# Ten of twelve column groups of the mixer's first product computed in channels, with standing weights

## The reference

```python
z = h @ w_in                                   # 256 x 2048 times 2048 x 6144
hy = dwconv3(z[..., :3072], hy_short_w, hy_short_b)
x0, x1, v = jnp.split(hy, 3, axis=-1)
y_a = x0 * two_sided_fftconv(v * x1, h_fwd, h_bwd, hy_bias)
gb, gc, xv = jnp.split(z[..., 3072:], 3, axis=-1)
y_b = gb * dwconv3(gc * xv, sc_conv_w)
return jnp.concatenate([y_a, y_b], axis=-1) @ w_out
```

## Time and profile before

| | us |
|---|---|
| median of 3 runs | 2268.76 (2268.59 to 2268.84) |
| span of the profiled execution | 2266.9 |
| TensorE busy | 2255.3 (99%) |
| VectorE busy | 1675.5 (74%) |
| ScalarE busy | 1332.9 (59%) |
| DMA read | 534.6 MB, 239 GB/s |

### The profile page before, as it was taken

One profiled execution on the slowest core, in us unless ns is written; L12 is line 12 of the kernel. 1 busy time (PEld: TensorE's weight loads), 2 busy tenths in 40 slices (PEclk: granted clock), 3 DMA queues, 4 the chain that ended last, 5 costly groups with the idle time before them and its releaser, 6 DMA issues.

```text
span 2266.9 us, 26633 instructions
## 1 busy us (share of the span) xinstructions
PE 2255.3 (99%) x10625; PEld 1873.7 (83%) x10625; DVE 1675.5 (74%) x2025; ACT 1332.9 (59%) x1775; POOL 104.5 (5%) x138
## 2 busy tenths in 40 slices
PE   9999999999999999999999999999999999999998
PEld 7778888888888888888888888888888888888887
DVE  6676864887788788787878788778788685456664
ACT  6455444766666666666666666666666564444443
POOL 0000000000000000000000000000000010000000
PEclk9999999999999999999999999999999999999999
DMA  9454455899998999886578999989888645643343
GB/s 358 167 174 162 164 186 186 289 291 272 287 303 265 277 292 267 283 282 236 219 281 240 287 289 261 285 281 277 270 281 258 240 152 223 244 172 149 148 163 116
DMA packets 77132, 542.63 MB, mean 239 GB/s; under 512 B 8682, under 2 KB 9013, under 8 KB 13968
## 3 DMA queue, kind: packets, MB, share of 16 engines
q1 hardware_dynamic: 61568, 429.58, 50.2%
q0 software_dynamic: 15296, 111.23, 22.7%
q10 hardware_dynamic: 144, 0.12, 0.0%
HBM read 534.60 MB, written 6.29 MB: 239 GB/s over the span
## 4 chain that ended last, share of the span: by engine, by line
PE 98%; DVE 2%; issue 0%; ACT 0%; ACTq 0%; POOLq 0%; POOL 0%
PE P L359 95%; PE P L362 3%; DVE low L626 0%; DVE R_h L614 0%; DVE R_f L611 0%; DVE R_f_r L611 0%; DVE R_g L614 0%; DVE X L614 0%; ACT R_h L502 0%; ACT EV L533 0%; DVE st L614 0%; DVE R_f L708 0%; ACT X L502 0%; DVE X L611 0%; ACTq L2710 0%
## 5 line engine op out<-in xcount | busy, mean ns | idle before, releaser
L626 DVE TENSOR_TENSOR low<-raw,hi 128x1024 fp32r<-128x1024 f32 (+3 forms) x694 | 813.4, 1200 | 290.7 <-ACT hi L507 286.4
L507 ACT ACTIVATE hi<-raw 128x1024 fp32r<-128x1024 f32 (+3 forms) x694 | 704.5, 1040 | 463.5 <-PE P L359 309.5
L359 PE MATMUL P<-hi,R_h 128*128 128x512 f32 (+2 forms) x2944 | 944.2, 392 | 0.6 <-DVE R_h L614 0.6
L359 PE MATMUL P<-hi,R_f_r 128*128 128x512 f32 x2480 | 791.4, 391 | 0.1
L359 PEld LDWEIGHTS P<-hi,R_h 128*128 128x128 f32 x2944 | 552.3, 188 | 116.4 <-issue 5.8
L359 PE MATMUL P<-low,R_h 128*128 128x512 f32 (+2 forms) x1472 | 570.2, 387 | 0.0
L359 PEld LDWEIGHTS P<-hi,R_f_r 128*128 128x128 f32 x2480 | 465.6, 188 | 96.3 <-DVE R_f_r L611 0.3
L359 PE MATMUL P<-low,R_f_r 128*128 128x512 f32 x1240 | 482.5, 389 | 0.0
L626 DVE TENSOR_TENSOR low<-R_f,hi 128x1024 fp32r<-128x1024 f32 x226 | 267.7, 1221 | 82.9 <-ACT hi L507 82.2
L359 PEld LDWEIGHTS P<-low,R_h 128*128 128x128 f32 x1472 | 276.7, 188 | 54.7 <-issue 2.6
L359 PEld LDWEIGHTS P<-low,R_f_r 128*128 128x128 f32 x1240 | 233.0, 188 | 47.1
(11 more groups left out here) (229 smaller groups left out, 1406.2 us busy)
## 6 DMA issues: line engine op xcount, KB each, us to landing
raw<-in_w_d SPq DMA_DIRECT2D x128, 1024.0 KB, 7.2
R_f<-in_w_u POOLq DMA_DIRECT2D x84, 1024.0 KB, 10.5
raw<-in_w_u SPq DMA_DIRECT2D x72, 1024.0 KB, 5.6
raw<-in_w_z SPq DMA_DIRECT2D x45, 1024.0 KB, 4.9
raw<-in_w_i SPq DMA_DIRECT2D x36, 1024.0 KB, 4.9
R_f<-in_w_u SPq DMA_DIRECT2D x28, 1024.0 KB, 6.9
X<-in_w_u SPq DMA_DIRECT2D x28, 1024.0 KB, 8.7
raw<-in_w_mo SPq DMA_DIRECT2D x16, 1024.0 KB, 4.9
```

Of the source, the lines that this page charges most:

```text
L359: return self.e.matmul(o, l, r, start=start, stop=stop, skip_group_check=True)
L507: self.e.activation(hi, raw, ACT.Copy).then_inc(*self.inc("high_made", ("high", k, d)))
L626: self.e.tensor_tensor(low, raw, hi.bitcast(f32), ALU.subtract).then_inc(*self.inc("low_made", *lows))
```

## The change

Groups 0 and 1 (gc) stay as they were, but `evac` multiplies with the square of the norm's factor, since xv then comes without one. For the other ten groups a weight tile holds one block of 128 columns over all 16 k (`laid_out`). `column_product` lets 128 x 128 pieces of the weights stand: for each k the high weights meet both parts of all tokens in one instruction of 512 columns (`H_both`: 256 of `HH`, 256 of `HL`), and the low weights meet the high part in one of 256. A tile fills one bank with channels on the partitions; its two halves have to be added. `column_pair` does two tiles. `gathered` copies the right halves to SBUF on ScalarE, adds the left ones on VectorE, and multiplies with `r_row`, the norm's factors along a row (not for xv). `r_row` is made once by `norm_diagonal` and `norm_spread` (two small products). No transposes of EV follow. `conv(..., apart=True)` issues the centre taps at once and the side taps one step later. A pair has four steps, two of which its own work takes.

```diff
+Z_ROWS = 2
+PAUSES = 1,
+    def column_product(self, b, wh, wl, j, ks, x_ready, free, *done):
+        m = self.m
+        o = m.P[b]
+        for k in ks:
+            self.wait_ge(x_ready)
+            self.wait_ge(("low", j, k // 4))
+            both, high = m.H_both[:, :, 256 * k:256 * k + 256], m.HH[:, k, :]
+            if k == 0:
+                self.wait_ge(free)
+            if k < 15:
+                self.mm(o[:, :], wh[:, k, :], both, k == 0, False)
+                last = self.mm(o[:, 0:256], wl[:, k, :], high, False, False)
+            else:
+                self.mm(o[:, 0:256], wl[:, k, :], high, False, False)
+                last = self.mm(o[:, :], wh[:, k, :], both, False, True)
...
+    def norm_spread(self, b, k, ready, free, done):
...
+        for t in range(2):
+            last = self.mm(m.P[b][:, 128 * t:128 * t + 128], m.EV[k][:, 256:384], m.EV[k][:, 128 * t:128 * t + 128], True, True)
...
 class Act(Engine):
+    def gathered(self, k, banks, row, ready, row_ready, free, done):
+        self.wait_ge(free)
+        for d, b in enumerate(banks):
+            self.wait_ge(ready[d])
+            self.copy(self.m.EV[k][:, 256 * d:256 * d + 256], self.m.P[b][:, 256:512], (done, "copied", d))
...
 class Dve(Engine):
+    def gathered(self, k, banks, row, ready, row_ready, free, done):
+        m = self.m
+        o = m.EV[k]
+        for d, b in enumerate(banks):
+            part = o[:, 256 * d:256 * d + 256]
+            self.wait_ge((done, "copied", d))
+            self.tt(part, m.P[b][:, 0:256], part, ALU.add, (done, "half", d))
+        if row is not None:
+            self.wait_ge(row_ready)
+            self.wait_ge((done, "half", 1))
+            z = v3(o[:, :], 2)
+            self.tt(z, z, row.unsqueeze(1).to_broadcast([128, 2, 256]), ALU.mult, done)
...
+    def column_pair(kind, c):
+        banks, products = pair(), []
+        for d in range(2):
+            j, wh, wl = take("w_z")
+            wh, wl = v3(wh, 16), v3(wl, 16)
+            done = ("product", j, 1)
+            for part, ks in enumerate((range(0, 4), range(4, 8), range(8, 12), range(12, 16))):
+                whose = {1: [("used", j, 0)], 3: [done, ("used", j, 1)]}.get(part, [])
+                E.column_product(banks[d], wh, wl, j, ks, list(h_m), bank_free[banks[d]], *whose)
+                if part in PAUSES:
+                    step()
+            products.append(done)
+            release(j, done)
+            step()
+        rest = []
+        later.extend([lambda: rest.append(mixer_columns(kind, c, banks, products)), lambda: rest[0]()])
...
     for n, kind in enumerate(kinds):
-        banks, done = gemm("w_z", HH, HL, h_m, 16, 512, steps=2)
-        flush()
+        if n < Z_ROWS:
+            banks, done = gemm("w_z", HH, HL, h_m, 16, 512, steps=2)
+            flush()
...
+            continue
+        for c in (0, 2):
+            column_pair(kind, c + 4 * (n % 2))
         if n == 7:
             flush_all()
-        ks, ms = evac(banks, done, scale_m=list(r1_m))
-        later += [nop] * {0: 4, 1: 1, 8: 1, 9: 1, 10: 1}.get(n, 0)
-        for c in (0, 2):
-            later.append(lambda kind=kind, c=c + 4 * (n % 2), ks=ks, ms=ms: mixer_turn(kind, c, ks, ms))
```

More of the change, by code:

```diff
@@ L746, in gate, with norm_diagonal @@
         self.tt(o, z, g, ALU.mult, done)
+    def gathered(self, k, banks, row, ready, row_ready, free, done):
+        m = self.m
+        o = m.EV[k]
[8 more added lines that the diff above has]
+            self.tt(z, z, row.unsqueeze(1).to_broadcast([128, 2, 256]), ALU.mult, done)
+    def norm_diagonal(self, k, ready, free, done):
+        m = self.m
+        self.wait_ge(free)
+        self.e.memset(m.EV[k][:, 256:384], 1.0).then_inc(*self.inc("dve_done"))
+        self.wait_ge(ready)
+        self.tt(m.r_square, m.R1, m.R1, ALU.mult, (done, "square"))
+        for t in range(2):
+            self.ts(m.EV[k][:, 128 * t:128 * t + 128], m.ident[:, :], m.R1[:, t:t + 1], None, ALU.mult, done)
     def v_times_k(self, fc, g, ks, ready, free, before, done):
@@ L1686, in conduct, with conv @@
     g0_m, g1_m = [None] * 8, [None] * 8
-    def conv(zs, dsts, ws, biases, ready, frees):
+    def conv(zs, dsts, ws, biases, ready, frees, apart=False):
         done = mark("conv")
         E.centre(zs, dsts, ws, biases, ready, frees, done)
+        ends = [(done, d) for d in range(len(zs))]
+        if apart:
+            return ends, lambda: E.side_taps(zs, dsts, ws, done)
         E.side_taps(zs, dsts, ws, done)
-        return [(done, d) for d in range(len(zs))]
+        return ends
     def gate(o, z, g, ready, free=None):
@@ L1697, in gate, with row_columns, norm_diagonal, norm_spread @@
         return done
-    def mixer_columns(kind, c, b, turned):
-        z = v3(P[b][:, :], 2)
+    def row_columns(c, b, turned):
+        done = mark("gc")
+        E.copy_out(G0[:, c:c + 2, :], v3(P[b][:, :], 2), turned, list(h_m), done)
+        g0_m[c] = g0_m[c + 1] = done
+        bank_free[b] = [done]
+    norm_m = {}
+    def norm_diagonal():
+        norm_m["k"] = k = ev(hold=True)
+        norm_m["diagonal"] = done = mark("diagonal")
+        norm_m["square"] = (done, "square")
+        E.norm_diagonal(k, [list(r1_m), id_m[1]], ev_free[k], done)
+    def norm_spread():
+        b, k, done = bank(), norm_m["k"], mark("spread")
+        norm_m["row"] = mark("row")
+        E.norm_spread(b, k, norm_m["diagonal"], bank_free[b], done)
+        let_go(k, done)
+        E.copy_out(m.r_row, P[b][:, 0:256], done, None, norm_m["row"])
+        bank_free[b] = [norm_m["row"]]
+    def mixer_columns(kind, c, banks, products):
+        k, done = ev(hold=True), mark("gathered")
+        by_row = kind != "xv"
+        E.gathered(k, banks, m.r_row if by_row else None, products, norm_m["row"], ev_free[k], done)
+        for d in range(2):
+            bank_free[banks[d]] = [(done, "half", d)]
+        whole = done if by_row else (done, "half", 1)
+        z = v3(EV[k][:, :], 2)
+        zs = [z[:, d, :] for d in range(2)]
         if kind in ("x1", "v", "x0"):
             base = {"x0": 0, "x1": 8, "v": 16}[kind]
-            zs = [z[:, d, :] for d in range(2)]
             ws = [[m.SW[n](base + c + d) for n in range(3)] for d in range(2)]
```

72 lines of the change are left out of this document (43 added, 29 removed).

## The result

| | before | after |
|---|---|---|
| median of the runs | 2268.77 us (2268.59 to 2268.84) | 2294.11 us (2292.99 to 2295.28) |
| span of the profiled execution | 2266.9 us | 2292.9 us |
| mean granted clock of TensorE | 0.999 | 0.994 |

The ratio is 1.0112 with a 95% interval of 1.0099 to 1.0125: 25.3 us slower. The forecast was 15.5 us slower, with a range up to 2291. The sign was right, the size was not, and the time lies outside the range. The four runs lie within 2.3 us; those of the kernel before lie within 0.25 us here, and within 0.5 to 1.7 us in the larger sets that stand beside the experiments, so that differences of 1 to 2 us between single runs say little.

The account below looks back on a forecast made before the run. TensorE's queue was taken as the bound, as long as VectorE and ScalarE deliver. On the 2266.9 us span, -4.6 + 14.7 + 5.4 = +15.5 gave 2282.4, plus 1.9 for the median: 2284 us, range 2271 to 2291.

Parts of the forecast that it names:

- TensorE's own work, -4.6: TensorE's queue in the mixer: 8.8 us of transposes less, 4.2 and 0.3 us added, a 0.3 us wait gone.
- The turns: Two turns of four transposes removed in each of ten groups, 20 x 0.44 us: 8.8 us saved on TensorE.
- the extra starts: 32 more product starts in each of ten groups, at 0.347 us a pair: +4.2 us in all.
- the operand in two runs: 512-column product reading two runs of 256: taken at the plain 0.227 us, at worst +8.4 us in all.
- (d): Rival: weight loads lie bare on TensorE's path, 60 us more, 2325 to 2345 us; chance 0.02.
- `norm_spread`, +0.3: Two added 128-column products on TensorE for the norm's row, 0.3 us with their start.
- The burst, +14.7: All four kernel transforms between tiles 31 and 32: TensorE waits for VectorE's kernel parts and banks, 14.7 us.
- The walk of the queues: VectorE's and TensorE's work timed item by item from tile 26, with idle VectorE pieces; gave the 14.7 us stall.
- `y_back`, +5.4: First `y_back` waits 4.9 us for the last spectrum product, and a bank ahead of it 0.4 us: 5.4 us.
- (a): Rival: VectorE and ScalarE keep up everywhere, only TensorE's own sum stays, 2264.2 us; chance 0.09.
- (b): Rival: the kernel transforms' burst costs 5.2 to 8.7 us and `y_back` nothing, 2269.4 to 2272.9 us; chance 0.14.
- (c): Rival: split tiles late in groups 6 to 11, or double-run product costs 8.4 us: 2291 to 2300 us; chance 0.07.

Follow-up runs that it names:

- e8: The kernel before the change, with each of the mixer's 24 turns of four transposes made twice into the same bank: 2279.13 us.
- e11: Changed kernel with `norm_spread`, first `y_back` and centre taps later, kernel transforms spaced out, and the last product of spectra one step later: 2266.94 us.
- e7: Changed kernel with the 512-column product reading one run (high parts of two k) in place of two runs of 256: 2292.42 us.
- e1: Changed kernel with `norm_spread` moved from the middle of tile 5 to the middle of tile 7, nothing else: 2289.42 us.
- e6: Changed kernel with ScalarE's centre taps issued together with the side taps, behind the next weight split in place of ahead of it: 2284.99 us.
- e5: Changed kernel with 34 idle TensorE products ahead of the second kernel transform and 29 ahead of the third: 2295.85 us.
- e3: Changed kernel with the first `y_back` moved back by two steps of the inserted work: 2293.61 us.
- e4: Changed kernel with `norm_spread` two tiles later, an added step per pair to bring kernel transforms one by one, and first `y_back` two steps later: 2278.80 us.

## Why the prediction was right or wrong

**What bounds the kernel, and the direction.** Right: TensorE's queue sets the time, and VectorE had no room where the change leans on it.

**TensorE's own work, -4.6.** Mis-sized: it is -2.7. The turns were priced right (8.8 forecast, 8.7 by e8). The pair of products was not: taken as 0.347 us, it is 0.352 or 0.353 in most tiles (5.65 us a tile in place of 5.55), so that the extra starts cost about 6 us (8.8 - 2.7) and not 4.2. The two products of `norm_spread` are in that figure: they are four records, and in e11 put the products behind them off by 0.45 us in place of the 0.3 forecast. I had named the operand in two runs as the unknown; e7 clears it. In the kernel before three products also come each 0.69 us in some stretches in place of the 0.68 of the earlier trace rows, so one pair of rows was too narrow a base. What makes them 1 to 2% slower is not settled; by e7 it is not the operand, and how busy the other engines are does not explain it.

The rival with bare weight loads (d) fell. The changed kernel's 640 loads for the 256-column products show 189 ns each in the page's groups, and a pair of products with its two loads comes each 0.352 us, less than its two loads laid end to end (0.378). The rule of the Trainium skill that the prediction quotes ("TensorE: Matmul & The Clock Gate"; it stands in the section "The mechanism") would have them bare; this trace disagrees. The same section also lets TensorE pull a load ahead when it goes to the background weight buffer, which the prediction left out.

**`norm_spread`, +0.3.** The failed step, worth 4.6 us. I priced its two products and did not ask when their operand is ready. With this step put right alone (e1, 2289.42 us) the time lies inside the forecast's range. In the kernel before TensorE needs nothing of the norm until the first turn at 43.41 us; `norm_spread` stands some 5 us ahead of that, and the diagonal is made at 40.3 us, because the tokens' transfer, their squares, GpSimd's and VectorE's small steps and two low parts come first. VectorE's rows:

```profile
36.22 0.16 DVE L687 TENSOR_REDUCE st<-st 128x2 f32<-128x8 f32 x1 [4.22 <-ACT EV L565]
...
37.90 2.35 DVE L664 TENSOR_TENSOR low<-raw,hi 128x1024 fp32r<-128x1024 f32 x2
...
40.33 0.47 DVE L657 TENSOR_SCALAR EV<-ident,st 128x128 f32<-128x128 f32 x2
```

**The burst, +14.7.** The walk of the queues was right to 0.2 us. Counted from the start of transform 1 (27.75 in the walk, 201.58 in the trace), transform 2 was due after 9.25 us and came after 9.33; transform 3 was due after 17.45 and came after 17.60; the pieces of 2 us were there, and e6 shows their cause. Then transforms 3 and 4 took 5.3 us and not the 2.7 of full speed, and tile 32 began slow: 17.5 in place of 14.7. e5 shows that this piece is the clock's. The forecast had no term for it anywhere.

**`y_back`, +5.4.** Close, by luck, since two errors stood against each other: VectorE was ready 81.8 us after the end of tile 32 (forecast 81.9), but TensorE came 0.9 us later than forecast, since its tiles are slower, so the wait was 3.9 and not 4.9; no bank was waited for ahead of it; and the slow clock added 2.4 us. What would cure it was not seen: a later `y_back` alone gains nothing (e3); the piece of VectorE's work has to move behind the adds (e11).

**The chances.** The case with everything hidden (a) and the one with half the burst (b) did not happen. (c) had the right time, 2291 to 2300, for a reason that did not occur: neither late low parts nor the operand, but the clock and `norm_spread`. Term by term, the mark is 9.8 us later than the sum had it (25.3 against 15.5): 4.6 at `norm_spread`, 2.8 in the burst, 0.9 at `y_back` and 1.9 in the products make 10.2. The last 0.4 us of difference are not accounted for. The two steps that failed are the readiness of `norm_spread`'s operand and a clock taken as full behind every wait; the latter alone is about 7 us of it (1.8, 2.8 and 2.4).

## What to carry to other kernels

A change that takes steps out of a loop also takes away the slots in which other work was placed: check where every inserted item now falls, for its operand (is it made yet?) and for its bank (who reads it, and behind what in that engine's queue?). If a wait appears, look at what stands in the queue of the engine waited for; moving the waiter alone may only hand the wait to the next one. And a wait of a few us on TensorE can cost more than its length: here 0.6 us of slow work came with each us waited at `y_back` and at `norm_spread`, and 0.3 in the burst, while waits of 2.24 us (e3), 2.51 us (e7) and 2.60 us (e4) cost their length alone.

## What the hardware showed that I had not expected

After TensorE had been idle from 203 us, its granted clock was 1.00 until 206 us, 0.92 in the next 2 us, and then 0.50. It rose behind transform 2, while TensorE waited again (0.87 and 0.98), fell back to 0.50 at 218 us, and was at 1.00 only from 226 us. With idle products in the gaps it stayed at 1.00 throughout. After shorter gaps the outcome varied between executions of the same order: 0.54 after 2.77 us, 1.00 after 2.51 us. What that is worth shows in e3, which is the same program as the changed kernel up to the first `y_back`: at tile 8 its execution is 2.0 us ahead, 0.5 of it a shorter wait, and at tile 32 it is 3.1 us ahead. The Trainium skill warns of this kind of loss ("TensorE: Matmul & The Clock Gate", section "HAM oscillation — how this bites in real kernels"): products that come after a wait run at the low clock, and the order of the work should keep TensorE fed. The trace agrees at three places, at 1.22 us for `norm_spread` in place of the 0.71 of e3 and e7, 2.90 in place of 1.53 for a transform, and 3.79 in place of 1.95 for a `y_back`.
